# A decoder trunk on one core: early bank reads, tanh gates, quarter-width norms and an even spread of branch A

## The reference, cut to what matters

```
Layer (pre-RMSNorm, adaLN shift/scale/gate from the conditioning vector c on every sub-layer):
  x += 1/2 * gate1 * SwiGLU(mod1(norm(x)))
  h  = mod2(norm(x)); z = h @ W_in
       A: chunked spatial-gating MLP, chunks of 128 positions, 4 channel groups, u * (tril(W_s) v + b)
       B: forgetting attention, 8 heads, QK-norm, logits + F_t - F_s with F = cumsum log sigmoid(f)
       C: mLSTM matrix memory, 4 heads, exponential input gate, sigmoid forget gate, max stabiliser
  x += gate2 * W_out( sum_b sigmoid(g_b) * (y_b @ W_branch_b) )
  x += 1/2 * gate3 * SwiGLU(mod3(norm(x)))

def rmsnorm(x, g):
    xf = x.astype(jnp.float32)
    y = xf * lax.rsqrt(jnp.mean(xf * xf, axis=-1, keepdims=True) + EPS)
    return (y * g.astype(jnp.float32)).astype(x.dtype)
```

## Time and profile before

| what | us |
|---|---|
| median of three runs | 3565.62 |
| the profiled execution, its own time | 3571.62 |
| its span | 3570.0 |
| PE busy | 3345.6 (94%) |
| DVE busy | 1062.5 (30%) |
| ACT busy | 750.9 (21%) |

### The profile page before, as it was taken

The page is one execution under the profiler, slowest core; times in us unless marked ns, Lnnn a source line. Parts: engine busy times, 40 slices in busy tenths (PEclk is TensorE's granted clock), DMA queues, the critical chain, the costliest instruction groups (busy, mean ns, idle before and its releaser), DMA issues.

```text
span 3570.0 us, 49432 instructions
## 1 busy us (share of the span) xinstructions
PE 3345.6 (94%) x21302; PEld 2776.3 (78%) x21302; DVE 1062.5 (30%) x1890; ACT 750.9 (21%) x1106; POOL 138.0 (4%) x269
## 2 busy tenths in 40 slices
PE   5999999989789998999989999999897899989999
PEld 4999986656557687999989999856655666879999
DVE  3333340132521114333343323320443211143333
ACT  2221212111441002221222212111124310022121
POOL 0000000002101100000000000000030020000000
PEclk9999999989999999999999999999999999999999
DMA  5344431201117621223223333221021284211221
GB/s 219 134 156 161 155 117 48 83 24 60 48 38 247 231 94 71 102 112 131 103 86 132 152 142 140 111 84 48 26 69 55 73 278 165 89 71 70 97 86 70
DMA packets 115403, 390.50 MB, mean 109 GB/s; under 512 B 12417, under 2 KB 62945, under 8 KB 96881
## 3 DMA queue, kind: packets, MB, share of 16 engines
q1 hardware_dynamic: 97152, 338.36, 26.0%
q0 software_dynamic: 14432, 34.09, 2.7%
q10 hardware_dynamic: 3600, 14.89, 1.1%
HBM read 373.60 MB, written 13.69 MB: 108 GB/s over the span
## 4 chain that ended last, share of the span: by engine, by line
PE 84%; DVE 7%; DMA 3%; ACT 3%; SPq 1%; issue 1%; ACTq 0%; DVEq 0%
PE g L697 75%; PE tb L697 4%; PE q L697 4%; DMA w<-in_w_up 1%; DVE area L1871 1%; DMA area<-in_cache_v 1%; DMA area<-in_w_ada 1%; ACT area L1454 1%; DVE area L1556 1%; DVE area L1548 1%; ACT L1301 1%; DVE area L1784 1%; DVE h_lo L1568 1%; DVE area L1557 0%; DVE w_lo L1599 0%
## 5 line engine op out<-in xcount | busy, mean ns | idle before, releaser
L697 PE MATMUL g<-h_hi,w_hi 128*128 128x272 f32 x2816 | 590.2, 291 | 55.2 <-DVE h_lo L1568 41.0
L697 PE MATMUL g<-h,w 128*128 128x272 f32 x2304 | 571.5, 403 | 36.0 <-DVE area L1854 23.0
L697 PE MATMUL g<-h_lo,w_hi 128*128 128x272 f32 x2816 | 591.1, 291 | 0.0
L697 PE MATMUL g<-h_hi,w_lo 128*128 128x272 f32 x2816 | 584.8, 289 | 0.0
L697 PEld LDWEIGHTS g<-h,w 128*128 128x128 f32 x2304 | 440.2, 194 | 161.7 <-issue 43.4
L1241 ACT ACTIVATE w_hi<-w 128x1024 fp32r<-128x1024 f32 (+2 forms) x240 | 274.2, 1144 | 1263.0 <-PE g L697 946.9
L697 PEld LDWEIGHTS g<-h_hi,w_hi 128*128 128x128 f32 x2816 | 443.0, 190 | 76.0 <-issue 36.1
L1599 DVE TENSOR_TENSOR w_lo<-w,w_hi 128x1024 fp32r<-128x1024 f32 (+2 forms) x240 | 319.3, 1332 | 513.7 <-ACT w_hi L1241 510.4
L697 PEld LDWEIGHTS g<-h_hi,w_lo 128*128 128x128 f32 x2816 | 448.9, 191 | 0.0
L697 PEld LDWEIGHTS g<-h_lo,w_hi 128*128 128x128 f32 x2816 | 446.5, 190 | 0.0
L697 PE MATMUL g<-area,w 128*128 128x272 f32 x1280 | 327.0, 411 | 50.8 <-ACT area L1301 47.0
(11 more groups left out here) (220 smaller groups left out, 2456.1 us busy)
## 6 DMA issues: line engine op xcount, KB each, us to landing
w<-in_w_up SPq DMA_DIRECT2D x44, 2048.0 KB, 8.1
w<-in_w_ada SPq DMA_DIRECT2D x32, 2048.0 KB, 8.0
w<-in_w_in SPq DMA_DIRECT2D x16, 2048.0 KB, 8.0
w<-in_w_down SPq DMA_DIRECT2D x16, 1536.0 KB, 6.8
w<-in_w_gate SPq DMA_DIRECT2D x48, 512.0 KB, 5.5
w<-in_w_down SPq DMA_DIRECT2D x16, 1280.0 KB, 5.6
area<-in_cache_k SPq DMA_DIRECT2D x72, 256.0 KB, 4.1
area<-in_cache_v SPq DMA_DIRECT2D x72, 256.0 KB, 4.0
```

The source lines that it names most:

```text
L697: return pe.matmul(o, a, b, start=start, stop=stop, skip_group_check=True, **kw)
```

## The change

It has four parts.

1. **When half units are read.** `due` becomes two lists: `early` (the half unit ended in an earlier step) and `late` (its bank is wanted again in this step). ACT reads the early ones at the top of a step in the mLSTM, the key norms and the attention; DVE does so in the attention, while in the key norms it reads both behind its reciprocal and multiply, as before. The `late` lists of the mLSTM, the key norms, the attention and the sample attention are empty with these tables.
2. **Gates as tanh.** The gate is read as tanh(x/2), and DVE forms (tanh+1) times the branch in one scalar_tensor_tensor. The factor 1/2 is put into the adaLN gate of the mixer.
3. **Norms on a quarter of the columns.** The four quarters of the tokens (136 columns) are summed by 32 products 32x136, each quarter into its own 32 partitions of one bank (`SUMS` in TB); root and reciprocal run over 128x136; DVE spreads the result to 128x544 with a mask that is zero outside the own quarter; two ones products (`norm_roots`) bring it to all partitions in TB; and DVE multiplies x by that, from PSUM. The first norm's squares, sums and roots stand ahead of the adaLN vectors.
4. **The table of branch A.** 8 blocks in each key norm and each step of the attention, in place of 4 and 10.

```diff
-        self.due, nxt = [], first
+        self.early, self.late, nxt = [], [], first
         for t in range(len(ticks)):
-            now = []
-            while nxt < last and (ends[nxt] < t or begins.get(nxt + 2, 10 ** 6) <= t):
-                now.append(nxt)
+            now = nxt
+            while nxt < last and ends[nxt] < t:
                 nxt += 1
-            self.due.append(now)
-        self.due.append(list(range(nxt, last)))
+            self.early.append(list(range(now, nxt)))
+            now = nxt
+            while nxt < last and begins.get(nxt + 2, 10 ** 6) <= t:
+                nxt += 1
+            self.late.append(list(range(now, nxt)))
...
-IN_FOX = Schedule(FILL_A, FILL_C, [4] * FOX_AT + [10] * 16 + [0])
+IN_FOX = Schedule(FILL_A, FILL_C, [8] * FOX_AT + [8] * 16 + [0])
...
-            def norm_sums():
-                p = unit()
-                product(p, [ones] * KD, lambda k: H[:, k, :], first=sq)
+            def norm_sums(ada_done):
+
+                if ada_done:
+                    pe.wait_ge(s_ada, ada_done)
+                for k in range(KD):
+                    wait(sq)
+                    for j in range(4):
+                        last = mm(SUMS[32 * j:32 * j + 32, :], ones[:, 0:32], H[:, k, j * QT:(j + 1) * QT],
+                                  k == 0, k == KD - 1)
+                last.then_inc(s_ns, 1)
+
+            def norm_roots(n, ada_done):
+
+                pe.wait_ge(s_ada, ada_done)
+                pe.wait_ge(s_rsx, n + 1)
+                for h in range(2):
+                    last = mm(TB[:, h, 0:HALF], ones, RS[:, h * HALF:(h + 1) * HALF], True, True)
+                last.then_inc(s_rs, 1)
...
-                p = mine()
-                ac.activation(halves(RS), both(p), ACT.Sqrt, bias=EPSC[:, 0:1], scale=1.0 / D).then_inc(s_rms, 1)
+            def roots(n):
+
+                ac.wait_ge(s_ns, n + 1)
+                ac.activation(RS4, SUMS, ACT.Sqrt, bias=EPSC[:, 2:3], scale=1024.0 / D).then_inc(s_rms, 1)
...
-                        ac.activation(GATE[what[-1]][:, cols], G[:, 2 + h, 0:HALF], ACT.Sigmoid, bias=ZERO[:, 0:1])\
-                            .then_inc(s_fa, 1)
+                        ac.activation(GATE[what[-1]][:, cols], G[:, 2 + h, 0:HALF], ACT.Tanh, bias=ZERO[:, 0:1],
+                                      scale=0.5).then_inc(s_fa, 1)
...
+            ac.wait_ge(s_x, 16)
+            squares()
+            roots(0)
             for n in range(FIRST_ADA):
                 rows(n)
-            ac.wait_ge(s_x, 16)
...
+                    read(l, IN_FOX.early[FOX_AT + it])
                     if it < 16:
...
-                    read(l, IN_FOX, FOX_AT + it)
+                    read(l, IN_FOX.late[FOX_AT + it])
...
-            def norm(part):
-                p = mine()
-                wait(t["rms"])
-                drained(ve.reciprocal(RS, RS), p)
-                ve.wait_ge(s_dr[p], un.d[p].value())
+            def inverse_roots(n):
+
+                ve.wait_ge(s_rms, n + 1)
+                link(ve.reciprocal(RS4, RS4))
+                ve.tensor_tensor(RS.rearrange("p (j c) -> p j c", j=4), RS4[:, None, :].to_broadcast([P, 4, QT]),
+                                 quarter[:, :, None].to_broadcast([P, 4, QT]), ALU.mult).then_inc(s_rsx, 1)
...
-                        link(ve.tensor_tensor(o, X[:, k, :], RS, ALU.mult))
+                        link(ve.tensor_tensor(halves(o), halves(X[:, k, :]), TB[:, :, 0:HALF], ALU.mult))
...
-                if kind == 2 and part != 1:
+                if kind == 2:
...
-                        ve.tensor_tensor(z, G[:, 2 + h, 0:HALF], GATE[b][:, cols], ALU.mult).then_inc(s_fd, 1)
+                        ve.scalar_tensor_tensor(z, GATE[b][:, cols], 1.0, G[:, 2 + h, 0:HALF], ALU.add, ALU.mult)\
+                            .then_inc(s_fd, 1)
```

More of the change, by code:

```diff
@@ L218, with ada_before @@
 LANDED = [16 * sum(parts(STREAM[j]) for j in range(i % 2, i + 1, 2)) for i in range(len(STREAM))]
+def ada_before(l, f):
+    before = STREAM[:AT["ffn", (l, f, 0)]]
+    return FIRST_ADA + sum(stage == "ada" for stage, _ in before)
 ADA_ORDER = [(0, i) for i in range(FIRST_ADA)] + [what for stage, what in STREAM if stage == "ada"]
@@ L357, in build @@
         PR, _ = take(T, start=o_f + 2 * T)
+        RS4, _ = take(QT, start=o_f + 2 * T)
         TN, _ = take(2, T, start=o_f + 3 * T)
@@ L1211, in store, with squares @@
                 ac.dma_start(dst, src).then_inc(s_outa, 16)
-            def norm(before_root=None):
+            def squares():
                 for k in range(KD):
@@ L1257, in chunk @@
                     split()
-                norm(first_splits)
+                if l or f:
+                    squares()
+                first_splits()
+                if l or f:
+                    roots(3 * l + 2 * f)
                 for k in range(KD):
@@ L1288, in tokens, with read @@
                 each(5, f)
-            def read(l, schedule, tick):
-                for u in schedule.due[tick]:
+            def read(l, units):
+                for u in units:
                     what, m, h = FILLS[u]
@@ L1317, in _ @@
                 ffn(l, 0)
-                norm()
+                squares()
+                roots(3 * l + 1)
                 each(4, lambda i, p: ac.activation(halves(YA[:, i, :]), both(p), ACT.Gelu_apprx_tanh,
@@ L1377, in _ @@
                         n = h * TILES + j
+                        read(l, IN_MLSTM.early[n])
                         a = COL[:, j * 12 + HB + h:j * 12 + HB + h + 1]
@@ L1386, in _ @@
                         last.then_inc(s_e, 1)
-                        read(l, IN_MLSTM, n)
+                        read(l, IN_MLSTM.late[n])
                     un.take()
@@ L1391, in _ @@
                 un.take()
-                read(l, IN_MLSTM, 16)
+                read(l, IN_MLSTM.early[16] + IN_MLSTM.late[16])
                 wait(t["stn"])
@@ L1402, in _ @@
                 last.then_inc(s_ses, 1)
-                read(l, IN_MLSTM, 17)
+                read(l, IN_MLSTM.early[17] + IN_MLSTM.late[17])
                 for hp in range(2):
                     un.take()
-                    read(l, IN_MLSTM, 18 + hp)
+                    read(l, IN_MLSTM.early[18 + hp] + IN_MLSTM.late[18 + hp])
                     wait(t["stn"])
@@ L1409, in _ @@
                 un.take()
-                read(l, IN_MLSTM, 20)
+                read(l, IN_MLSTM.early[20] + IN_MLSTM.late[20])
                 wait(t["stn"])
@@ L1413, in _ @@
                 wait(t["yc"])
-                read(l, IN_MLSTM, 21)
+                read(l, IN_MLSTM.early[21] + IN_MLSTM.late[21])
                 ac.wait_ge(s_outa, outs.value())
@@ L1432, in _ @@
                 for m in range(8):
+                    read(l, IN_FOX.early[m])
                     if m < 7:
@@ L1442, in _ @@
                                   scale=1.0 if m < 4 else 1.0 / DB).then_inc(s_rtn, 1)
[L1443 removed]
+                    read(l, IN_FOX.late[m])
                 ac.wait_ge(s_qkr, 8 * (l + 1))
@@ L1468, in _ @@
                 ac.activation(YB[:, 3, 0:NP], G[:, 1, :], ACT.Copy).then_inc(s_ybc, 1)
-                read(l, IN_FOX, FOX_AT + 17)
+                read(l, IN_FOX.early[-1])
                 def exps(g):
@@ L1842, in _, with read @@
                 ve.sem_inc(s_lff, 1)
-                def read(schedule, tick):
-                    for u in schedule.due[tick]:
+                def read(units):
+                    for u in units:
                         what, m, h = FILLS[u]
@@ L1873, in _ @@
                                             ALU.mult, ALU.mult).then_inc(s_qkr, 1)
-                    read(IN_FOX, m)
+                    read(IN_FOX.early[m] + IN_FOX.late[m])
                 ve.wait_ge(s_qkr, 8 * (l + 1))
@@ L1883, in _ @@
                     w = (i + 1) * P
+                    read(IN_FOX.early[FOX_AT + it])
                     if it < 16:
@@ L1942, in own @@
                                    G[:, g, 0:64].rearrange("p (k t) -> p k t", k=4)).then_inc(s_ybs, 1)
-                read(IN_SAMPLE, SAMPLE_PRE)
+                read(IN_SAMPLE.early[SAMPLE_PRE] + IN_SAMPLE.late[SAMPLE_PRE])
                 for n in range(QUADS):
@@ L1947, in _ @@
                         maxima(0)
-                        read(IN_SAMPLE, SAMPLE_MID)
+                        read(IN_SAMPLE.early[SAMPLE_MID] + IN_SAMPLE.late[SAMPLE_MID])
                         sums(0)
@@ L1953, in _ @@
                         masked(0)
-                    read(IN_SAMPLE, quad_tick(n))
+                    read(IN_SAMPLE.early[quad_tick(n)] + IN_SAMPLE.late[quad_tick(n)])
                     if n == 2 * PAGES:
@@ L1959, in _ @@
                 masked(1)
-                read(IN_SAMPLE, quad_tick(QUADS))
+                read(IN_SAMPLE.early[-1])
                 own(1)
                 for tick in range(3):
-                    read(LAST_MERGE, tick)
+                    read(LAST_MERGE.early[tick] + LAST_MERGE.late[tick])
```

61 lines of the change are left out of this document (41 added, 20 removed).

## The result

The changed kernel takes 3475.44 us (median of four runs, 3473.31 to 3482.63), the one before 3565.27; the ratio is 0.9753, with a 95% interval of 0.9733 to 0.9773. Forecast were 3487.

| stage (layer 0, layer 1) | before | after | difference | forecast |
|---|---|---|---|---|
| start to the first feed-forward product | 58.98 | 49.65 | -9.3 | -9.6 |
| norm ahead of the mixer | 13.8, 13.8 | 11.3, 11.3 | -2.5 each | -3.1 each |
| norm behind the out projection | 15.9, 15.9 | 13.8, 13.8 | -2.1 each | -2.7 each |
| norm of layer 1's first half FFN | 16.0 | 15.4 | -0.6 | -1.4 |
| key norms | 41.18, 40.85 | 59.67, 60.10 | +18.5, +19.3 | +21 each |

A forecast was written before the change was run, and what follows sets the result against it. PE's row of products was taken to set the end. Per layer 48.8-21=27.8, twice 55.6, plus norms 22.6, made 78 us less: 3571.6 to 3493.4 profiled, 3487 against the median; range 3450 to 3530.

The forecast's parts named there:

- Norms: All norms outside the key norms, narrowed to a quarter of the columns: gain 5.4+6.2+1.4+9.6=22.6 us, bounds 13 to 26.
- The first norm: Start of the program: squares, sums and roots move into waits for the first weights; gain 9.6 us (8.5 to 11.5).
- the other three: Norms behind out projection, ahead of mixer, and of layer 1's first half FFN: gains 2.7, 3.1 and 1.4 us each.
- The upper bound: Norm behind the out projection: first multiply at 1384.7 to 1385.5; 3.5 to 4.2 us from load to multiply reused elsewhere.
- Key norms: Key norms, per layer: 64 blocks instead of 32 and two longer waits, 62.1 us against 41.2, +21 (+15.5 to +26).
- covered gate waits: Key norms: 1.4 us of gate waits that stepping through the queues showed covered, taken off the stage's sum.
- Rival (b): Key norms find their waits hidden, +15.5 us each: total 3476; chance 0.07.
- rival (d): Key norms: a switch of tables costs twice its load of 1.28 us, 6 per layer: total 3499; chance 0.03.
- Attention: Attention, per layer: blocks 15.5, waits 27.1 and clock 6.2 saved, 48.8 us, from 156.0 to 107.2; bounds 40 to 52.
- rival (a): Half of the attention's waits stay, 14 us per layer back: total 3515; chance 0.15.
- (c): Attention stays at 156 us, paced by its own chain, while key norms grow: total 3585, slower; chance 0.05.
- the clock: Attention: 7.8 us lost at granted clock 0.95; 6.2 come back, 1.6 behind the first scores' wait stay.

The follow-up runs named there:

- the last kernel: Changed kernel with, in the key norms, DVE's branch reads ahead of the reciprocal and ACT's gate reads behind the root: 3444.76 us, ratio 0.9635.

## Why the prediction was right

The time came out 11.6 us below the forecast, within the range; the terms are compared in the table above. The misses partly offset each other: the attention gave 9.8 us more than forecast and the key norms cost 4.2 less, the norms gave 3.5 less.

**Norms**: 19.1 of a forecast 22.6. The places were right, and the old norms put back give the old stages. The first norm gave 9.3 of 9.6; the other three lie just below their own ranges (2.1 of 2.3 to 3.1, 2.5 of 2.8 to 3.5, 0.6 of 1.0 to 1.7), by one and the same term. The chain from root to first multiply behind the out projection is 4.5 us (1328.86 to 1333.37), where the forecast had 3.5 to 4.2 between the load's end and the multiply. The two roots products ran at the lower clock (2.15, the upper bound taken was 1.9), and the bounds were averaged though the row before them was an idle PE. The upper bound was also added up too short: 0.4+1.0+0.73+1.9 and 0.4 of hand-overs are 4.4.

**Key norms**: +18.5 and +19.3 of +21. Two waits of 6.45 and 5.71 at m = 3 and 6 (forecast 6.7 and 6.7), a slow stretch behind each (2.7 to 2.8 us, forecast 2.0), a last wait of 2.43 (3.4). The sum took off 1.4 for covered gate waits that are not among the waits it adds up, and no row shows that term; what the trace shows is that no wait on a gate is left, and that the three waits come to 14.6. Rival (b), waits that hide, and rival (d), a switch of twice its load, are both out: the loads are still 1.28, and the ring explains the stage.

**Attention**: -53.8 and -53.6 of -48.8, beyond the step's upper bound of 52. The waits went whole, so rival (a) is out, and so is (c): PE is busy 99% of the stage. Term by term: PE stood for 28.2 us and stands for 1.1, which is the 27.1 of the forecast. The 32 blocks come to 15.3 at the undisturbed 3.83 us for 8, forecast 15.5. The undersized term is the clock. Read in windows of 1 us, what the granted clock leaves out of PE's busy time is 8.4 us in the kernel before, 1.7 in the changed kernel with the table of before, and 0.0 in the changed kernel. The step had put 6.2: it went by the mean clock of 0.95, 7.8, and kept 1.6 of slow start, which did not occur. These three make 50.8. The other 3.0 are in PE's busy time too (26.6 less, of which blocks and clock are 23.7), about 0.2 for each of the 14 stops that went; what they are is not shown.

**A right number for a reason that was half wrong.** The step said that the waits go because the gates are read at the top, because tanh shares exp's table, and because PE comes back to the bank a step later. The runs show that the first is enough without the one or without the other. Tanh is worth nothing once the reads are early (102.30 against 102.28), and so is the later use of the bank (10 blocks a step run free of waits as well). Early reads without both at once were not run. With late reads both help but do not suffice: the table alone takes the attention from 156.0 to 136.7 us, of which the moved blocks are 15.3, and tanh takes it on to 124.8. The prediction also missed what the table does: it booked the blocks' move as neutral and the ring in the key norms as its price, but never set the two against each other, and in this change the move loses 2 us a layer.

## What to carry to other kernels

A read that frees a bank belongs at the first point of its engine's stream at which its data is sure to be there, ahead of the step's own long work; here this took away what waits the attention had left. With tanh gates and the even table most of that was DVE's (19.7 of 22.5 us), while in the kernel before the longer waits were ACT's (21.5 against 5.6). It need not be the top of the step: in the key norms ACT's gate reads, ahead of the root, waited for PE's product, and the stage got 4 to 6 us shorter with them behind the root. Before filler work is moved into a stage, look for a ring in it: here PE, DVE and ACT each waited for the next, and the moved work lengthened this stage by 18.5 us, and with the attention's gain counted in it lost 2 us a layer. After the reads had changed places on two engines it paid 14. Take the parts of a change back one by one even when the sum comes out: of the four parts here, tanh brought nothing beside early reads and the table lost a little.

## What the runs showed of the hardware

The length of a stop does not say by itself how the products behind it run. A stop of 1.44 us left the next 16 records at 3.93, one of 2.17 made them 5.33, both in the key norms of one kernel, and in its layer 1 one of 2.20 made them 6.94; behind 6.45 and 5.71 in the changed kernel they took 6.50 and 6.67. A stop of 2.43 us ahead of the attention's first scores was followed by 5.57 in layer 0 of that kernel, and by 3.88 in the changed kernel. With stops of 0.9, 1.0 and 1.5 us in the key norms of the last kernel the granted clock of the stage was 1.00.

Products 32 wide in four column groups took 1.84 us for 56 records of 136 columns, 0.033 each. Full-width ones took 7.50 for 32 records of 272, 0.117 for each 136 columns: 3.6 times as long for the same sums. A narrow product alone is not faster: 44 wide, in one group, 32 records of 272 columns took 7.53 (`g<-h,wfi`, in the kernel before and in the changed ones).
